# A fused two-layer encoder trunk on one core: the second attention in another order, with GpSimd rotating the last queries and ScalarE making the probability sums

## The reference

```python
def mla_mixer(h, w_in, q_lora_norm, kv_lora_norm, w_uq, w_ukv, q_norm, k_norm, w_out, cos, sin):
    z = h @ w_in
    c_q, c_kv, k_rope = jnp.split(z, (C_Q_RANK, C_Q_RANK + C_KV_RANK), axis=-1)
    q = (rms_norm(c_q, q_lora_norm) @ w_uq).reshape(B, S, C_HEADS, C_QK)      # 16 heads of 96
    kv = (rms_norm(c_kv, kv_lora_norm) @ w_ukv).reshape(B, S, C_HEADS, C_NOPE + C_V)
    k_nope, v = jnp.split(kv, (C_NOPE,), axis=-1)                             # 64 and 64
    k = jnp.concatenate([k_nope, broadcast(k_rope)], axis=-1)                 # 64 + 32
    q, k = rms_norm(q, q_norm), rms_norm(k, k_norm)
    q, k = (concat([s[..., :C_NOPE], apply_rope(s[..., C_NOPE:], cos, sin)]) for s in (q, k))
    out = dense_chunk_causal_attention(q, k, v, C_QK ** -0.5)   # chunks of 64, softmax over the keys
    return out.reshape(B, S, C_OUT) @ w_out
```

## Time and profile before

| what | value |
|---|---|
| median of three runs | 1231.43 us |
| the profiled execution's own time | 1233.23 us |
| its span in the trace | 1231.4 us |
| TensorE busy | 1202.1 us, 98% |
| TensorE weight load, VectorE, ScalarE, GpSimd busy | 595.1, 526.0, 338.7, 54.1 us |
| longest shares of the chain that ended last | L2620 40%, L2630 19%, L2080 to L2082 7% each |
| HBM read | 411.02 MB, 335 GB/s over the span |

### The profile page before, as it was taken

The page is one execution under the profiler, slowest core; times in us unless marked ns, Lnnn a source line. Parts: engine busy times, 40 slices in busy tenths (PEclk is TensorE's granted clock), DMA queues, the critical chain, the costliest instruction groups (busy, mean ns, idle before and its releaser), DMA issues.

```text
span 1231.4 us, 21710 instructions
## 1 busy us (share of the span) xinstructions
PE 1202.1 (98%) x9398; PEld 595.1 (48%) x9398; DVE 526.0 (43%) x1081; ACT 338.7 (28%) x676; POOL 54.1 (4%) x68
## 2 busy tenths in 40 slices
PE   9989999999989999999999999999999999999997
PEld 7768888888778623333433333334333333333332
DVE  6976666555776411331331142143142133313323
ACT  7575554544876200110220020012010011101101
POOL 3400000000420000000000000000000000000000
PEclk9999999999999999999999999999999999999999
DMA  9513455453616899999999999999999999999995
GB/s 369 191 38 139 172 195 181 176 194 124 259 47 241 375 397 389 413 371 429 426 428 427 427 428 427 428 425 387 430 426 427 428 427 427 427 424 428 428 427 229
DMA packets 40278, 413.54 MB, mean 336 GB/s; under 512 B 4848, under 2 KB 5360, under 8 KB 9840
## 3 DMA queue, kind: packets, MB, share of 16 engines
q1 hardware_dynamic: 39888, 412.00, 81.6%
q10 hardware_dynamic: 288, 0.09, 0.0%
HBM read 411.02 MB, written 1.05 MB: 335 GB/s over the span
## 4 chain that ended last, share of the span: by engine, by line
PE 87%; DVE 4%; DMA 3%; ACT 3%; issue 1%; POOL 1%; SPq 0%; DVEq 0%; ACTq 0%; POOLq 0%
PE PS L2620 40%; PE PS L2630 19%; PE PS L2080 7%; PE PS L2082 7%; PE PS L2081 7%; DMA arena<-in_expert_tiles 3%; PE PS L2493 2%; PE PS L2197 1%; ACT arena L921 1%; PE PS L2152 1%; PE PS L2525 1%; DMA ring<-in_dense_tiles 1%; PE PS L2101 1%; DVE w_split L1346 1%; DVE arena L1437 0%
## 5 line engine op out<-in xcount | busy, mean ns | idle before, releaser
L2620 PE MATMUL PS<-homes,arena 128*32 128x512 f32 x3192 | 351.6, 593 | 2.9 <-DVE arena L1974 1.7
L2620 PEld LDWEIGHTS PS<-homes,arena 128*32 128x32 f32 x3192 | 103.1, 110 | 240.8 <-issue 232.7
L1967 DVE SCALAR_TENSOR_TENSOR arena<-arena,PS 64x256 f32<-64x256 f32 x126 | 52.1, 414 | 377.0 <-ACT arena L1282 375.0
L2630 PE MATMUL PS<-homes,arena 128*32 128x512 f32 x1896 | 208.8, 592 | 0.0
L1282 ACT ACTIVATE arena<-PS 64x512 f32<-64x512 f32 x63 | 37.2, 590 | 460.5 <-PE PS L2620 460.5
L2080 PE MATMUL PS<-w_split,hT_hi 128*128 128x512 f32 (+2 forms) x372 | 142.3, 382 | 4.1 <-DVE w_split L1346 1.9
L2081 PE MATMUL PS<-w_split,hT_hi 128*128 128x512 f32 (+2 forms) x372 | 139.6, 375 | 0.0
L2082 PE MATMUL PS<-w_split,hT_lo 128*128 128x512 f32 (+2 forms) x372 | 139.5, 375 | 0.0
L2630 PEld LDWEIGHTS PS<-homes,arena 128*32 128x32 f32 x1896 | 61.3, 110 | 139.9 <-issue 139.3
L2620 PE MATMUL PS<-arena 128*32 128x512 f32 x936 | 103.8, 592 | 0.0
L1348 DVE SCALAR_TENSOR_TENSOR w_split<-ring,gains,w_split 128x512 fp32r<-128x512 f32 (+3 forms) x116 | 77.7, 730 | 18.4 <-ACT w_split L863 18.3
(11 more groups left out here) (235 smaller groups left out, 1029.7 us busy)
## 6 DMA issues: line engine op xcount, KB each, us to landing
homes<-in_expert_tiles SPq DMA_DIRECT2D x109, 2048.0 KB, 20.4
ring<-in_dense_tiles SPq DMA_DIRECT2D x49, 1024.0 KB, 4.8
free_homes<-in_expert_tiles SPq DMA_DIRECT2D x17, 2048.0 KB, 21.2
arena<-in_expert_tiles SPq DMA_DIRECT2D x16, 2048.0 KB, 20.1
homes<-in_expert_tiles SPq DMA_DIRECT2D x24, 1024.0 KB, 18.9
arena<-in_expert_tiles SPq DMA_DIRECT2D x18, 1024.0 KB, 22.1
x_res<-in_expert_tiles SPq DMA_DIRECT2D x4, 1024.0 KB, 13.7
ring<-in_dense_tiles SPq DMA_DIRECT2D x6, 512.0 KB, 5.8
```

Of the source, the lines that this page charges most:

```text
L1967: ins = v.scalar_tensor_tensor(out=act_exp[64 * j:64 * (j + 1), g, :], in0=gate[0:64, g, c], scalar=1.0, in1=PS[0:64, gu_banks[k][g], c], ...
L2620: ins = pe.matmul(PS[GROUP * q:GROUP * (q + 1), gu_banks[k][g], :], xT[:, cc, o + g * GROUP:o + (g + 1) * GROUP], quarter(k_home, q), star ...
L2630: ins = pe.matmul(PS[GROUP * q:GROUP * (q + 1), 3 + g, :], tokens_T(k, c, q // 2, g), quarter(k_home, q), start=k == 0 and c == 0, stop=end)
```

## The change

The scores start before the keys and queries of block 1 are transposed. TensorE transposes keys and queries of block 0, makes the scores of steps 0 and 1, then transposes the keys of block 1, and the queries of block 1 in two halves: groups 0 and 1 after step 0's transposes, groups 2 and 3 after step 2's values. Scores of step 4 follow step 1's transposes, those of step 5 step 3's. On ScalarE the exponentials of step 4 now stand ahead of the copies of step 2 (`copies(2)`); its main loop begins at step 3, and the high halves move to steps 3, 4, 5 and 6, while VectorE's low halves keep their places. VectorE rotates the queries of block 0 ahead of the second keys, with the sum of squares inside the rotation. GpSimd rotates the queries of block 1 (four instructions), behind its third `rsqrt` and ahead of its fourth. Every exponential of the second attention returns its sum, the eight `tensor_reduce` of `back` go, and steps 0 to 3 have a probability buffer each. `keep_clock` goes from the first four steps. The banks of the transposed groups are renamed to match.

```diff
-FILL = {"AB": (9, 3, 3, 3, 7), "C": (3, 3, 3, 3, 1)}
+FILL = {"AB": (9, 3, 3, 3, 7), "C": (0, 0, 0, 0, 1)}
...
-LAST_QUERY_BANKS = (0, 1, 6, 7)
+HEAD_BANKS = {(0, 0): (0, 1, 2, 3), (0, 1): (4, 5, 6, 7), (1, 0): (2, 3, 4, 5), (1, 1): (0, 1, 6, 7)}
...
-HI_AHEAD = {"AB": {}, "C": {0: (0, 0), 3: (0, 1), 4: (1, 0), 5: (1, 1)}}
+HI_AHEAD = {"AB": {}, "C": {3: (0, 0), 4: (0, 1), 5: (1, 0), 6: (1, 1)}}
...
         def probs_of(kind, i):
 
             if kind == "C" and i < 4:
-                o = 512 * (i % 2)
-                return arena3[:, o:o + 512].rearrange("p (s m n) -> p s m n", s=2, m=2)
+                part = (arena3[:, 0:512], arena3[:, 512:1024], hflat[:, 1024:1536], rope_tmp)[i]
+                return part.rearrange("p (s m n) -> p s m n", s=2, m=2)
...
-            for r in range(R_KQ1, R_NORM3):
+            for r in range(R_KQ1, R_KQ1 + NT + 1):
                 rsqrt(r)
+            zt = q1[1].rearrange("p (s n) -> p s n", n=C_QK)
+            tmp = rope_tmp.rearrange("p (s n) -> p s n", n=C_ROPE)
+            cos, sin = tab1[0][:, 1, 0:C_ROPE], tab1[0][:, 1, C_ROPE:]
+            pool.wait_ge(q_evac, 6)
+            pool.wait_ge(qk_normed, 6)
+            link(pool.tensor_tensor(tmp[:, :, 0:half], zt[:, :, C_NOPE + half:], bc(sin[:, 0:half], 1, C_HEADS), ALU.mult))
+            link(pool.tensor_tensor(tmp[:, :, half:], zt[:, :, C_NOPE:C_NOPE + half], bc(sin[:, half:], 1, C_HEADS),
+                                    ALU.mult))
+            pool.wait_ge(q_squared, 2)
+            link(pool.tensor_tensor(zt[:, :, C_NOPE:], zt[:, :, C_NOPE:], bc(cos, 1, C_HEADS), ALU.mult))
+            pool.tensor_tensor(zt[:, :, C_NOPE:], zt[:, :, C_NOPE:], tmp, ALU.add).then_inc(last_rotated, 1)
+            rsqrt(R_KQ1 + NT + 1)
...
-                    if i >= 2:
-                        before = 4 if kind == "C" and i == 4 else i - 1
-                        a.wait_ge(probs_transposed, s0 + 2 * before)
-                        if kind == "C":
-                            a.wait_ge(probs_summed, before)
+                    if kind == "C" and i == 3:
+                        a.wait_ge(last_rotated, 1)
+                    elif kind == "C" and i == 5:
+                        a.wait_ge(qk_transposed, 24)
+                    elif i >= 2 and not (kind == "C" and i == 2):
+                        a.wait_ge(probs_transposed, s0 + (4 if kind == "C" and i == 4 else 2 * i - 2))
...
-                                               accum_out=sm[:, 8 + o:9 + o] if kind == "AB" else None)
+                                               accum_out=sm[:, 8 + o:9 + o])
...
+                def first_steps():
+
+                    transposed_heads(1, 0, range(2))
+                    copies(0)
+                    transposed_heads(1, 1, range(1))
+                    exps(2)
+                    copies(1)
+                    exps(3)
+                    exps(4)
+                    copies(2)
+                    transposed_heads(1, 1, range(2, 3))
...
-                for j in range(8):
-                    copy_probs(2 * j)
-                    copy_probs(2 * j + 1)
-                    if kind == "C" and j == 2:
-                        last_heads()
-                    elif j + 2 < 8:
-                        if kind == "C" and j == 3:
-                            exps(4)
+                if kind == "C":
+                    first_steps()
+                for j in range(3 if kind == "C" else 0, 8):
+                    copies(j)
+                    if j + 2 < 8:
                         exps(j + 2)
                     if j in HI_AHEAD[kind]:
...
             transposed_heads(0, 0, range(3))
+            transposed_heads(0, 1, range(3))
             query_squares(1)
-            transposed_heads(1, 0, range(3))
-            transposed_heads(0, 1, range(2))
-
-            a.wait_ge(ms_ready, R_KQ1 + 2 * NT)
-            transposed_heads(0, 1, range(2, 4))
...
+                if between:
+                    between()
                 link(v.tensor_tensor(s[:, :, lead:], s[:, :, lead:], bc(cos, 1, nh), ALU.mult))
                 return v.tensor_tensor(s[:, :, lead:], s[:, :, lead:], tmp, ALU.add)
...
                     if kind == "C":
-                        v.tensor_reduce(fields[:, 2], probs_of(kind, i).rearrange("p s m n -> p m s n"),
-                                        AX.X, ALU.add).then_inc(probs_summed, 1)
-                        v.wait_ge(probs_summed, i + 1)
                         link(v.reciprocal(rinv[:, t, 4 * j:4 * j + 4].rearrange("p (s m) -> p m s", s=2), fields[:, 2]))
...
-                    for i in range(3):
-                        front(i)
+                    front(0)
+                    transposed_heads(0, 1, 3)
+                    front(1)
+                    query_sums(1)
+                    transposed_heads(1, 0, 2)
+                    transposed_heads(1, 0, 3)
+                    front(2)
                     back(0)
                     front(3)
-                    query_heads(1)
+                    transposed_heads(1, 1, 1)
                     back(1)
+                    query_scales(1)
+                    front(4)
+                    final(0, 0)
                     back(2)
-                    final(0, 0)
-                    transposed_heads(1, 1)
-                    query_scales(1)
+                    transposed_heads(1, 1, 3)
                     back(3)
-                    front(4)
+                    front(5)
                     final(0, 1)
-                    front(5)
...
+            def query_heads(t, between):
+                v.wait_ge(q_evac, 3 * t + 3)
+                rotated = rotate(q1[t], C_HEADS, C_QK, C_NOPE, half, tab1[0][:, t, 0:C_ROPE], tab1[0][:, t, C_ROPE:],
+                                 between)
                 return rotated.then_inc(qk_normed, 1)
...
             key_heads(0)
-            query_sums(0)
+            query_heads(0, lambda: query_sums(0))
+            transposed_heads(0, 0, 3)
             key_heads(1)
-            transposed_heads(0, 0)
-            query_heads(0)
-            query_sums(1)
-            transposed_heads(1, 0)
             query_scales(0)
...
-                    if kind == "C" and i < 4:
-                        pe.wait_ge(qkT_ready, 11 + i)
-                        if i == 3:
-                            pe.wait_ge(qkT_copied, 6)
+                    if kind == "C" and i < 3:
+                        pe.wait_ge(qkT_ready, 8 + i)
+                    elif kind == "C" and i == 3:
+                        pe.wait_ge(qkT_copied, 6)
+                    elif kind == "C" and i < 6:
+                        pe.wait_ge(qkT_ready, 9 + i)
+                        pe.wait_ge(qkT_copied, 5 + i)
                     elif i >= 2:
-                        before = {4: 2, 5: 4}.get(i, i - 1) if kind == "C" else i - 1
-                        pe.wait_ge(exp_done, s0 + 2 * before)
+                        pe.wait_ge(exp_done, s0 + 2 * i - 2)
...
                         pe.wait_ge(probsT_ready, s0 + i - 1)
+                    elif kind == "C":
+                        pe.wait_ge(qkT_ready, 11 + i)
...
+                    if kind == "C" and i == 0:
+                        pe.wait_ge(qkT_copied, 8)
...
+                    heads(1, 0)
+                    scores(2)
+                    scores(3)
+                    step(0)
+                    pe.wait_ge(exp_done, s0 + 4)
+                    pe.wait_ge(last_rotated, 1)
+                    heads(1, 1, range(2))
+                    outputs(0)
+                    step(1)
+                    scores(4)
+                    outputs(1)
+                    step(2)
+                    outputs(2)
+                    pe.wait_ge(exp_done, s0 + 8)
+                    heads(1, 1, range(2, 4))
+                    step(3)
+                    scores(5)
+                    outputs(3)
+
                 scores(0)
                 scores(1)
                 if kind == "C":
-                    scores(2)
-                    scores(3)
-                for i in range(8):
+                    first_steps()
+                for i in range(4 if kind == "C" else 0, 8):
 
                     if i < len(FILL[kind]):
                         keep_clock(2, FILL[kind][i])
-                    if i + 2 < 8 and (kind == "AB" or i > 3):
+                    if i + 2 < 8:
                         scores(i + 2)
-                    transposes(2 * i)
-                    transposes(2 * i + 1)
-                    if kind == "C" and i == 3:
-                        pe.wait_ge(qkT_ready, 17)
-                        scores(4)
+                    step(i)
...
-                    values(2 * i)
-                    values(2 * i + 1)
-                    if kind == "C" and i == 2:
-                        between()
-                    if kind == "C" and i == 3:
-                        pe.wait_ge(qkT_copied, 7)
-                        scores(5)
+                    outputs(i)
...
```

(64 more changed lines are left out.)

22 lines of the change are left out of this document (9 added, 13 removed).

## The result

| | median | runs |
|---|---|---|
| before | 1231.59 us | 1231.17 to 1232.98 |
| changed | 1241.38 us | 1239.51 to 1242.31 |

The ratio is 1.0076, with a 95% interval of 1.0061 to 1.0091: slower by 9.8 us, where 1233.8 (1228.3 to 1236.6) was forecast. The profiled execution took 1240.59 us with a span of 1238.8, against 1233.23 and 1231.4: 7.4 us more, and its parts can be read row by row.

A forecast was written before the change was run, and what follows sets the result against it. In the attention a loop of four engines was taken to bind, its end shifting the full experts one to one. Links +1.6 and clock +0.8 gave +2.4, 1233.8 us; range 1228.3 to 1236.6.

The forecast's parts named there:

- The end follows the attention: Attention's end through the projection to the experts' start: a shift reaches the kernel's end one to one, in both directions.
- The start: VectorE ahead of the first scores: first query transposes 3.1 to 3.2 us earlier, front(0) at 345.8.
- TensorE's gaps: Idle of some 3.3 us near 359, with copies(2) behind four exponentials, and 2.9 us near 382.
- Fronts: Front(5) to front(7): front, exponentials, high half and low half run in series, 6.3 us a step, twice.
- GpSimd's four instructions: Rotation of block 1's queries on GpSimd: 0.7 and 1.3 us, 4.0 in all, from 345.2 to 349.4.
- The sums: Exponentials returning sums: 0.35 us a step, four times from front(4) on, 1.4 us, contained in the path's total.
- the late fall: TensorE's clock drop between 380 and 390 us, 1.5 us of work lost: taken to recur at no new cost.
- one more in the middle: A second clock fall in the attention's middle: 0 to 1.5 us, half taken, +0.8.
- the second rival: From the idle near 359, TensorE's clock falls and stays down into step 5: +4 to +5.5, 1235.4 to 1236.9; 0.16 with the fourth.
- The links: The attention's four-engine loop priced link by link, up to the values of step 6: +1.6.
- The block of VectorE by GpSimd: Two-input VectorE instructions beside GpSimd's rotation: a whole instruction's block would cost 0 to 1.3 us; taken as 0.
- the 0.7 us that I subtracted: Same prices on the old order put step 6's values at 383.4, 0.7 late, so this came off the sum.

The follow-up runs named there:

- e5: The changed kernel with the eight probability sums back on VectorE and exponentials returning nothing: 1238.72 us, ratio 1.0062.
- e1: The changed kernel with unused TensorE products filling its two long gaps, twelve behind step 2's transposes and five behind step 6's: 1235.2 us, ratio 1.0029.
- e9: The kernel of e8 with three filling products in its one long gap, behind step 6's transposes: 1228.62 us, ratio 0.9973 to the kernel before.
- e6: The kernel before without the twelve filling products ahead of steps 0 to 3, all else as it was: 1233.51 us, ratio 1.0015.
- e7: The kernel before with the probability sums made by ScalarE and the eight reduces gone from VectorE: 1234.93 us, ratio 1.0023.
- e10: The kernel of e9 with the probability sums back on VectorE and exponentials returning nothing: 1229.95 us, ratio 0.9982 to the kernel before.
- e11: The kernel of e9 with the queries of block 1 rotated by VectorE instead of GpSimd: 1233.53 us, ratio 1.0016 to the kernel before.
- e2: The changed kernel with the last two query groups transposed ahead of step 2's values, and step 5's scores ahead of step 3's transposes: 1237.93 us, ratio 1.0052.
- e8: The changed kernel, no fills, with last queries and step 5's scores earlier, copies(2) and a query copy before step 4's exponentials, first high half after step 3's: 1231.2 us.

## Why the prediction was wrong

**What held.** The end follows the attention nearly one to one: the release moved by 6.84 us, the span by 7.4. The start: front(0) 3.08 us earlier from query_sums(0), 3.1 to 3.2 forecast. TensorE's gaps of 3.29 and 2.89 for 3.3 and 2.9, and their cause, copies(2) behind four exponentials. Fronts 6.37 us apart for 6.3, each behind a low half that had waited for its high half, 2.69 and 3.29 us. GpSimd's four instructions 0.92, 0.75, 1.27 and 1.26 us, 4.2 for 4.0, over at 349.76. The sums at 0.35 a step in the last steps (e5).

**The step that failed is the clock's.** I let the late fall recur "at no new cost", allowed one more in the middle, and put it at 0 to 1.5 us, half of that taken: +0.8. The changed kernel fell four times, from 353, 364, 377 and 387 us, the last for twice as long as in the kernel before; 17.1 us at 1.2 GHz in place of 3.4. e1, which differs from it in the fills alone, took 6.2 us less. Two things were wrong in the reasoning. I looked at the two longest gaps, and there are two more, of 2.17 us ahead of step 0's transposes and of 2.00 ahead of step 4's values: four gaps, and a fall at each: the first three 0.3 to 1.8 us behind the end of the gap, the fourth within it. (It isn't the gap alone: in e1 the one of 2.00 remained, the work before it was denser, and no fall followed.) And I priced a fall by the work that it slows inside one stretch, as if the loop could hide half; but a fall comes at a gap, when TensorE's values and transposes are what ScalarE and VectorE wait for: the copy of a query group idled 2.40 us for the transposes behind the second fall, 1.36 in e1. From the changed kernel to e1 13.7 us less at 1.2 GHz gave 4.3 us of the stage, 0.31 us for each.

Executions of one kernel can be set beside this price. Of the 29 of the kernel before beside e9, twelve had a granted clock of 0.999 over the span and seven 0.996; their medians are 1230.4 and 1232.9 us, 2.5 us for some 7.4 us more at 1.2 GHz (by the clocks as rounded), 0.33 for each. The changed kernel's give less: two with 0.986 and 0.985, where the profiled one had 0.991, took only 1.6 and 1.7 us longer. So 0.31 is a price of these places and not of the clock. Nor is all of the 6.2 us between the medians seen in the stage: 4.3 are, and the profiled execution of the changed kernel lies 0.8 under its median.

So the bound of the second rival, too, was too narrow: its mechanism and its place were right, but it reached one fall further, to 1236.9, and not to four. It was too low by its own terms as well: transposes, scores and values of 0.95, 1.89 and 1.0 us, doubled, add 3.8 us, of which it counted 0.8 and 1.5.

**The links.** Forecast +1.6; measured +3.6 by e1's ratio, and +3.56 at front(7) by the table. Three differences of 0.5 to 0.7 us add up to about the missing 2.0. The block of VectorE by GpSimd, taken as 0, was 0.53 and 0.65 us, the second on the path: VectorE's list from front(0) to the copy for scores(4) took 10.1 us, not 9.6. The first fall, which e1 keeps, held scores(4) another 0.7 us behind that copy (356.15 to 356.87). And the 0.7 us that I subtracted, because my prices run late on the old order, should not have come off: the same prices were not late on the new one. That one is inferred from what the other two leave; no run tests it.

The Trainium skill, "SBUF — State Buffer", section "Who interferes with whom", has the rule that I weighed and set aside for one row of the old trace: a VectorE instruction that uses its second port and a GpSimd instruction that reads SBUF exclude each other, to the end of the one that came first. The two rows above agree with it: both VectorE instructions end within 0.03 us of GpSimd's. The bias has two SBUF inputs; the scale has one and not two, as the prediction had it, and the page counts such an instruction in where it runs in a 2-port mode, which no row here shows apart from the block itself.

The row for which the rule was set aside was no test of it: L1757 began at 341.22 and GpSimd's instruction at 341.39, so VectorE was the first. Nor does every GpSimd instruction block, which is narrower than the rule: in the changed kernel a bias at 353.93 took its 0.16 us within GpSimd's power of 2.91 us, from 351.74 on.

The Trainium skill, "TensorE: Matmul & The Clock Gate", section "HAM oscillation — how this bites in real kernels", says that idle gaps of TensorE let its clock drop, which spoke against removing the fills. e1 and e6 agree with it, in the new order and in the old; but the length of a gap alone doesn't decide here. In e6 the clock fell with gaps of no more than 1.34 us ahead of it in the steps, and in e1 one of 2.00 us was followed by no fall.

**What is not settled.** Whether e7's 1.0 to 2.2 us at like clock are the sums alone. And the first fall, which every kernel of the new order has, some 13 to 14 us behind query_sums(0), in e10 and e11 some 18: a fill in the gap ahead of it wasn't tried. Bank 0 was free for one: it holds the scores of step 0, and the changed kernel's exponentials had read them by 349.15 us, ahead of the gap from 350.14 to 352.31.

## What to carry to other kernels

Before filling work is removed from an engine whose clock can fall, look for every gap that remains, and price each as a fall of its own on the links right behind it, not as one in common. When a list is reordered, follow each instruction that moved past another on its engine to whoever waits for it: here copies behind exponentials and halves one step late took back 5.6 us of the 6.7 that the earlier scores had won. And test an order with the clock held, by fills in its gaps; else the one effect hides the other, as in e2.

## What the runs showed of the hardware that was not expected

Small changes of TensorE's work moved long stretches of its clock. With the fills of 0.95 us gone from the old order, one execution had ten microseconds at 1.2 GHz in one piece (e6), and with scores(4) 0.9 us later another had thirteen (e11). In the other direction 1.46 us of products that do nothing gave back 3.3 us of a stage (e8 to e9). A sum returned by an exponential shows as an instruction of its own, 0.2 us each, and lengthens the pitch of exponentials of 256 elements by 0.09. A VectorE instruction of 0.16 us took 0.81 beside a GpSimd sum and 0.16 beside a GpSimd power.
